# A 64-byte shift of the rounded weights' buffer in SBUF, with the small tables laid out anew

## The reference, cut to what matters

```
x = layer_norm(ALPHA * x + h, ln_g[i, 0], ln_b[i, 0])
x = layer_norm(ALPHA * x + memory_cross_attention(x, mem, ...), ...)
x = layer_norm(ALPHA * x + conv_glu(x, ffn_w_in[i], ..., ffn_w_out[i]), ...)
...
h_lat = h_lat + g1 * y_lat
h_lat = h_lat + g2 * swiglu(modulate(rmsnorm(h_lat, norm_ffn_g[i]), sh2, s2), ffn_w_in[i], ffn_w_out[i])
```

## The kernel before, in words

| tensor | before | after |
|---|---|---|
| `ring`, `w_lo` | A | A |
| `x_lo` (on `tri`), `s_lo`, `wdt2` | A | A |
| `arena` and in it `x_hi`, `m_hi`, `m_lo`, `h_hi`, `h_lo`, `s_hi`, `w_half`, `w_swo` | B | B |
| `w_hi` (in `arena`) | B | A |
| `xlat`, `mod`, `sc_in`, `row`, `small` | B | A |
| `pt`, `lnrow`, `dist`, `tri`, `x`, `xt2` | A | A |

## Time and profile before

### The profile page before, as it was taken

How to read it: one execution, slowest core, us unless ns; L and a number is a source line. 1 busy time by engine, 2 the same in 40 slices (tenths; PEclk the granted TensorE clock), 3 DMA queues, 4 the chain that set the end, 5 groups by cost and what they waited for, 6 DMA issues and landing times.

```text
span 2034.1 us, 33951 instructions
## 1 busy us (share of the span) xinstructions
PE 1919.6 (94%) x13633; PEld 1703.3 (84%) x13633; DVE 1077.8 (53%) x1502; ACT 996.0 (49%) x1703; POOL 1255.3 (62%) x585
## 2 busy tenths in 40 slices
PE   7989999999999989999998899999889999999997
PEld 7889798987999966879987787877679988959996
DVE  5472246633610073135557645688539943947971
ACT  4654345543444362436653444478645545535542
POOL 8758466687888503648896334100569886318995
PEclk9999999999999999999999899999999999988999
DMA  7335377774555534435552222344345554224552
GB/s 263 144 126 206 104 274 304 306 273 166 187 188 187 194 139 163 187 145 186 187 195 100 83 83 83 127 164 166 106 153 186 186 186 148 102 83 172 189 186 103
DMA packets 49218, 342.32 MB, mean 168 GB/s; under 512 B 5264, under 2 KB 7312, under 8 KB 8144
## 3 DMA queue, kind: packets, MB, share of 16 engines
q1 hardware_dynamic: 47440, 331.02, 45.1%
q0 software_dynamic: 1664, 9.70, 1.3%
HBM read 339.65 MB, written 1.05 MB: 167 GB/s over the span
## 4 chain that ended last, share of the span: by engine, by line
PE 73%; DVE 10%; POOL 6%; ACT 6%; issue 4%; DMA 1%; DVEq 0%; POOLq 0%; SPq 0%; ACTq 0%
PE bank L1831 13%; PE bank L1774 11%; PE bank L1768 11%; PE bank L1771 11%; POOL w_lo L2339 4%; PE bank L1881 3%; PE bank L1811 2%; PE bank L1809 2%; PE bank L1806 2%; PE bank L1353 2%; PE bank L1355 2%; PE bank L1356 2%; PE bank L1587 2%; DVE arena L765 2%; ACT arena L1181 1%
## 5 line engine op out<-in xcount | busy, mean ns | idle before, releaser
L2339 POOL TENSOR_TENSOR w_lo<-ring,w_hi 128x1024 fp32r<-128x1024 f32 x404 | 983.7, 2462 | 299.6 <-ACT w_hi L2949 281.4
L1768 PE MATMUL bank<-x_hi,w_hi 128*128 128x256 f32 x2176 | 613.9, 282 | 16.4 <-POOL w_lo L2339 13.0
L1774 PE MATMUL bank<-x_lo,w_hi 128*128 128x256 f32 x2176 | 619.1, 284 | 0.0
L2949 ACT ACTIVATE w_hi<-ring 128x1024 fp32r<-128x1024 f32 x448 | 448.8, 1052 | 293.4 <-DMA ring<-slabs_dram 284.1
L1771 PE MATMUL bank<-x_hi,w_lo 128*128 128x256 f32 x1824 | 511.5, 280 | 0.0
L1768 PEld LDWEIGHTS bank<-x_hi,w_hi 128*128 128x128 f32 x2176 | 414.6, 191 | 27.2 <-issue 27.2
L1774 PEld LDWEIGHTS bank<-x_lo,w_hi 128*128 128x128 f32 x2176 | 413.9, 190 | 0.0
L1771 PEld LDWEIGHTS bank<-x_hi,w_lo 128*128 128x128 f32 x1824 | 348.1, 191 | 0.0
L2871 ACT ACTIVATE arena<-bank 128x512 f32<-128x512 f32 (+1 forms) x179 | 98.3, 562 | 278.8 <-PE bank L1774 190.1
L458 POOL TENSOR_TENSOR w_lo<-ring,w_half 128x1024 fp32r<-128x1024 f32 x32 | 78.1, 2444 | 113.3 <-ACT w_half L1069 113.3
L2339 POOL TENSOR_TENSOR w_hi<-ring,w_hi 128x1024 fp32r<-128x1024 f32 x44 | 104.4, 2395 | 47.9 <-ACT w_hi L2949 47.9
(11 more groups left out here) (365 smaller groups left out, 3685.0 us busy)
## 6 DMA issues: line engine op xcount, KB each, us to landing
ring<-slabs_dram SPq DMA_DIRECT2D x308, 1024.0 KB, 4.8
lnrow<-ln_dram POOLq DMA_DIRECT2D x6, 1024.0 KB, 6.5
arena<-slabs_dram SPq DMA_DIRECT2D x4, 1024.0 KB, 8.0
xt<-xT_dram SPq DMA_DIRECT2D x1, 1024.0 KB, 5.7
xt<-memT_dram SPq DMA_DIRECT2D x1, 1024.0 KB, 11.8
x<-x_dram SPq DMA_DIRECT2D x1, 1024.0 KB, 13.6
arena<-ctx_dram POOLq DMA_DIRECT2D x1, 1024.0 KB, 7.1
lnrow<-ln_dram POOLq DMA_DIRECT2D x2, 512.0 KB, 4.7
```

Source lines behind the costliest of these rows:

```text
L1768: ins = pe.matmul(dst, wh[:, k, c], src[0][:, k, :], start=(k == 0 and (ch == 0 or not both)), stop=False, skip_group_check=both)
L1774: ins = pe.matmul(dst, wh[:, k, c], src[1][:, k, :], start=False, stop=(k == KC - 1), skip_group_check=both)
L2339: pool.tensor_tensor(dst[:, c], ring[:, s, c], w_hi[:, s, c].bitcast(F32), ALU.subtract).then_inc(S["lo_ready"], 1)
L2949: a.activation(w_hi[:, g % RING, c], ring[:, g % RING, c], ACT.Copy) \
```

## The change

`pt` moves behind `xlat`, `small` behind `arena`; `arena` grows by 16 elements and `small` shrinks by 16; a few columns of `small` change places (`pick`, `lamp`, `dtn`, `dcol`). `w_hi` begins 20496 instead of 20480 elements behind the start of `arena`, 64 bytes further on. The tensors of the table above keep their half but for `w_hi` and the small ones. No instruction is added, removed or moved on any engine, and no semaphore changes; what changes is addresses alone.

```
         x = sb("x", [P, NT, D])
         xt2_at = aligned()
         xt2 = sb("xt2", [P, KC, 2 * T])
-        xT = xt2[:, :, T:2 * T]
-        sideT = xt2[:, :, 0:T]
...
         lnrow = sb("lnrow", [P, 2, D])
-        pt = sb("pt", [P, NPT])
         row = sb("row", [P, NROW])
-        small = sb("small", [P, 544])
         mod = sb("mod", [P, 2, 6, 8, 2])
         sc_in = sb("sc_in", [P, KC * 32 + 30])
         xlat = sb("xlat", [P, KC, T])
+        pt = sb("pt", [P, NPT])
         arena_at = aligned()
-        arena = sb("arena", [P, 28672])
+        arena = sb("arena", [P, 28688])
+        small = sb("small", [P, 528])
+        xT = xt2[:, :, T:2 * T]
+        sideT = xt2[:, :, 0:T]
...
-        pick = small[:, 256:288]
+        pick = small[:, 232:264]
...
-        lamp = small[:, 288:416]
-        dtn = small[:, 288:544].rearrange("p (t h) -> p t h", t=4)
+        lamp = small[:, 264:392]
+        dtn = small[:, 264:520].rearrange("p (t h) -> p t h", t=4)
...
-        dcol = small[:, 232:248]
+        dcol = small[:, 56:72]
...
         w_lo = part("w_lo", ring_at, RING, SLAB)
-        w_hi = part("w_hi", arena_at + 4 * 20480, RING, SLAB)
+        w_hi = part("w_hi", arena_at + 4 * 20496, RING, SLAB)
```

## The result

The changed kernel takes **2041.4 us** (median of 19 runs, 2036.5 to 2046.5) against 2033.9 for the kernel before (19 runs, 2032.4 to 2035.9): a ratio of 1.0038, 95% interval 1.0031 to 1.0045. The forecast was 2044.5. Sign and size are right. The rule that gave them is not, and most of what follows is about that. Note also the spread: 10 us where the kernel before has 3.5.

A forecast was written before the change was run, and what follows sets the result against it. TensorE was taken as the bound: matmul count times distance of starts. T form +12.0, N form -1.7 and the rest 0 made +10.3 us on 2034.2, so 2044.5 us; 8-of-10 range 2021 to 2058.

The forecast's parts named there:

- What bounds the kernel: Steady stretches: TensorE always busy at full clock; time is matmul count times distance of starts, which only new addresses can change.
- T form: Split-product triples at L1768, L1771, L1774, 256 columns: 5472 matmuls go from 115.6 to 117.8 ns, +12.0 us.
- N form: Split-product triples with the moving side now all in half A: 768 matmuls go from 120.0 to 117.8 ns, -1.7 us.
- f0 and the memory's products: Split products of stage f0 and of the memory, T and N form: stay at 117.8 ns, 0 us.
- the first rival: Moving operand in the same half as the next stationary one costs time: -9.1 us, 2025.1 us; chance 0.34.
- Rows form: 512-column split products at L1831, 1344 matmuls: taken as 0, with -3.0 us to as much more as bounds.
- Everything else: Small tables in plain float32 products, vector work, scalars, ACT and POOL: costed at nothing; POOL up to +5 us.
- I choose by what they have in common: Split-product triples: one side constantly in one half gives 117.8 ns, as in three earlier stretches; chance 0.37.
- second: Equal halves of a moving operand and the stationary one before it help: T form 120.0 ns, +29.8, 2064.0 us; chance 0.13.
- The third: Nothing changes, as the five stretches differ for another reason than addresses modulo 128: 2034.2 us; chance 0.12.
- The fourth: Only POOL's subtraction (L2339) gets slower, by up to 6%: 2039 us; chance 0.04.
- What would make it wrong: A T form distance below 115.6 ns or differing between slabs, meaning more address bits count than were read out.

The follow-up runs named there:

- second profile: The changed kernel run and profiled once more without an edit; 2044.5 us.
- the map: No kernel computation: TensorE alone runs T form triples at 64 sets of operand places modulo 256, 96 matmuls each, in two passes; its time is not to be compared.
- tables only: The changed kernel with w_hi back at its old offset in the arena, so every split operand keeps its old half; 2044.6 us, 1.0047 to the kernel before.
- V2: The changed kernel with pt and row ahead of tri, sc_in behind the arena: w_hi at 0, w_lo at 128, tokens at 192 modulo 256; 2019.0 us, ratio 0.9933.

## Why the prediction was right, and where its reasons were not

- **What bounds the kernel, and that only the distance of starts can move:** right. Counts, order and busy shares stayed; nothing else in the trace has a price.
- **T form, +12.0 us (117.8 for all):** the value is there, in 57% of the distances; 43% have 119.3. By the mean of 118.4 the term is 5472 x 2.8 = +15.3. The prediction had 119.3 only as the upper bound of its range, from the earlier trace rows.
- **N form, -1.7:** right, 117.8.
- **f0 and the memory's products, 0:** f0 went to 119.3 and 117.7 in turn, 1056 x 0.5 = +0.5. The memory's went down by 1.3 us together, with 113.4 or 113.5 ns in part of its stretches. 113.4 is the distance that the first rival had for them, but not by its reason.
- **Rows form, 0, bound -3.0:** by the starts 231.2 before and 228.9 ns after, 1344 x -2.25 = -3.0. It fell on the bound. The prediction's 232.2 divides a row of the chain with its pauses.
- **Everything else, 0:** POOL, yes. The plain product L1881, yes, but not by what was read: 592 ns is a duration, and a duration does not show the distance (L1771 has 280 ns in the T form and in f0 alike in the earlier trace rows, with 115.6 and 117.9 ns between starts). The starts of L1881 are 429 ns apart in steady rows, by `tri` and by `arena`, before and after. The state-space stage's products on w_half, no: -1.2 in the 256-column part, from an address bit that I had not looked at.
- **The sum:** 15.3 - 1.7 + 0.5 - 1.3 - 3.0 - 1.2 = +8.6 against +7.5 of the medians, and +10.3 forecast. The terms that I had at 0 took back what the T form cost more, which is luck. The profiled execution shows only +3.4, chiefly because L1639 and the plain products of L1980 were 2.8 and 1.7 us shorter in it: 5 and 1 of their 64 ran at half granted clock, where it had been 33 and 9. In the second profile L1639 has 2.6 of that back.
- **The step that failed** is "I choose by what they have in common": five stretches, sorted by halves modulo 128. A rule on halves was fitted to five values, three of which were alike. The table of addresses was at hand, and a column modulo 256 would have shown that the change moves the arena by 128. I took the change's own words (places modulo 128) for the list of what could matter. That the T form came out near 117.8 is luck: it is the commonest value of the map (28 of 64 cells in both passes), and one constant side does not give it: with w_hi and w_lo in one half, as the rule wants it, the 32 cells range from 113.3 to 121.1.
- **The rivals:** the first and second fall with tables only, as the forecast's rule does. The first was said to decide if the T form stayed under 116.2 ns, where 3 us of loss and the gains elsewhere balance; against its own gains of 9.1 us the balance is at 117.3, so that line was drawn wrong. The third, that nothing changes, had 2034.2, and falls with 1.0038. The fourth falls with the earlier trace rows against 2407 ns.
- **What would make it wrong** was named: a T form that "differs between slabs, since then more bits of the address count than I have read out of these rows". That happened. It had two causes, though: more bits, and, at the same addresses, the entry (shown with TensorE alone).

The Trainium skill, page "SBUF — State Buffer", section "Who interferes with whom", has TensorE with two independent read ports, waiting on nobody. The runs with TensorE alone show that no other engine is needed for the loss, and in them the distance of starts goes from 113.3 to 120.0 with nothing but the distance of the two operands' addresses. By two independent ports it would not move; here the measurement decides.

**Open:** why a pair has the value that it has, why some have two, and why mixed pairs do not add up. That the reads of the moving operand and of the next weights meet somewhere in 256 bytes is an argument; no run shows the place where they meet. That nothing is lost at half clock fits it, and does not show it.

## What to carry to other kernels

Where TensorE streams split products back to back at full clock, the start addresses of its two operands are worth some per cent of the stretch (113.3 to 120.0 ns for one pair here, and 0.7% of this kernel): read the distance of starts in a long stretch, compare it with columns over clock, and list the places of all operands modulo 256, relative to each other. Of the four distances in steps of 64 bytes, a pair of 256 columns was best with the moving operand 192 bytes further on than the stationary one (though with 117.8 in some entries), one of 512 columns with both at the same place; for mixed products measure a map with TensorE alone, several entries for each set, and prefer a set with one value over one with a better least value. A change that "only moves tables" is a change of every address behind them: compute the addresses, and don't stop at the modulus which the change names.

## What the hardware showed that I had not expected

- One pair of addresses, 256 columns: 120.0, 117.8, 118.6, 113.3 ns at distances of 0, 64, 128, 192 bytes modulo 256, where the columns alone would take 106.7. No set of places reached 106.7; the least was 113.3.
- 512 columns: 226.7, 228.9, 232.3, 233.3 at the same distances, against 213.3.
- 128 columns: 111.7 ns at each of the four distances.
- At half granted clock the T form takes 213.3 ns, its columns alone, with the places of before and of V2 alike: the loss is there at full clock only.
- The same instructions at the same addresses can run at 117.8 or at 119.3, or at 113.3 or at 117.8, for a whole stretch of 96 to 1040 matmuls, by how the stretch is entered.
- The plain float32 product of L1881 and POOL's subtraction show none of it: 429 ns between starts with either operand and in both kernels, and a median of 2416 against 2407 ns.
